# Mixing stage: the triangular inverse kept packed by blocks of 32 up to step 16, its products in four column groups of TensorE, and all spreading copies on ScalarE

## What is computed

```python
def step(state, inp):
    r_t, k_t, v_t, w_t, a_t, b_t = inp
    sa = jnp.einsum('bhvk,bhk->bhv', state, a_t)
    state = state * w_t[:, :, None, :] + sa[..., None] * b_t[:, :, None, :] + v_t[..., None] * k_t[:, :, None, :]
    return state, jnp.einsum('bhvk,bhk->bhv', state, r_t)
```

## Time and profile before

| | us |
|---|---|
| Median of 3 runs | 2895.5 |
| Lowest and highest run | 2890.79, 2899.98 |
| The profiled execution: its own time | 2889.8 |
| The profiled execution: its span | 2888.0 |
| Mean granted clock of PE over the span | 0.97 of full speed |

### The profile page before, as it was taken

One profiled execution on the slowest core, in us unless ns is written; L12 is line 12 of the kernel. 1 busy time (PEld: TensorE's weight loads), 2 busy tenths in 40 slices (PEclk: granted clock), 3 DMA queues, 4 the chain that ended last, 5 costly groups with the idle time before them and its releaser, 6 DMA issues. The chain is left out here.

```text
span 2888.0 us, 38654 instructions
## 1 busy us (share of the span) xinstructions
PE 2693.2 (93%) x14472; PEld 2220.4 (77%) x14473; DVE 1942.9 (67%) x2438; ACT 1350.8 (47%) x1914; POOL 577.5 (20%) x487
## 2 busy tenths in 40 slices
PE   8999988889988879999999699999999899999998
PEld 7988767777776758888888588766677688888887
DVE  4441167777764579999999663586778888887314
ACT  5111155555543257777777452236654334333312
POOL 0000035655550010000000330130000343341000
PEclk9999989999998979999999799999999999999999
DMA  6456111111006459999999631001031222223314
GB/s 205 177 191 251 74 58 54 44 37 36 28 9 232 185 208 408 408 412 409 408 411 368 208 110 47 22 1 60 1 111 63 62 87 87 80 80 116 136 48 160
DMA packets 166286, 439.86 MB, mean 152 GB/s; under 512 B 21852, under 2 KB 102800, under 8 KB 152848
## 3 DMA queue, kind: packets, MB, share of 16 engines
q1 hardware_dynamic: 151552, 384.13, 36.2%
q0 software_dynamic: 8848, 33.03, 3.0%
q10 hardware_dynamic: 5760, 20.97, 1.8%
HBM read 358.93 MB, written 79.17 MB: 152 GB/s over the span
## 5 line engine op out<-in xcount | busy, mean ns | idle before, releaser
L134 PE MATMUL psum<-part,expert_x_high 128*128 128x512 f32 x520 | 207.5, 399 | 2.9 <-issue 1.5
L136 PE MATMUL psum<-part,expert_x_low 128*128 128x512 f32 x520 | 203.8, 392 | 0.0
L134 PE MATMUL psum<-project_w_high,high 128*128 128x448 f32 (+1 forms) x512 | 194.4, 380 | 4.0 <-DVE low L398 4.0
L136 PE MATMUL psum<-project_w_high,low 128*128 128x448 f32 (+1 forms) x512 | 193.5, 378 | 0.0
L135 PE MATMUL psum<-project_w_low,high 128*128 128x448 f32 (+1 forms) x512 | 193.5, 378 | 0.0
L129 DVE TENSOR_TENSOR expert_down_low<-expert_down,expert_down_high 128x2048 fp32r<-128x2048 f32 x62 | 139.3, 2288 | 39.6 <-ACT expert_down_high L124 39.6
L971 POOL TENSOR_TENSOR mix_ab_step<-mix_abrb,mix_pair_mask 128x512 f32<-128x512 f32 x80 | 115.4, 1467 | 182.8 <-ACT mix_abrb L1106 182.4
L129 DVE TENSOR_TENSOR expert_gate_low<-expert_gate,part 128x2048 fp32r<-128x2048 f32 x64 | 143.9, 2289 | 10.0 <-ACT part L124 8.5
L134 PE MATMUL psum<-part,ffn_w_high 128*128 128x512 f32 x352 | 139.9, 397 | 11.4 <-DVE ffn_u L4172 6.3
L129 DVE TENSOR_TENSOR expert_up_low<-expert_up,part 128x2048 fp32r<-128x2048 f32 x64 | 143.8, 2289 | 1.0 <-ACT part L124 1.0
L135 PE MATMUL psum<-ffn_b_low,ffn_w_high 128*128 128x512 f32 x352 | 138.9, 395 | 0.0
(11 more groups left out here) (728 smaller groups left out, 7567.2 us busy)
## 6 DMA issues: line engine op xcount, KB each, us to landing
expert_gate<-in_w_gate_dram SPq DMA_DIRECT2D x32, 2048.0 KB
expert_up<-in_w_up_dram SPq DMA_DIRECT2D x32, 2048.0 KB, 10.2
expert_down<-in_w_down_dram SPq DMA_DIRECT2D x32, 2048.0 KB, 10.9
ffn_w<-in_ffn_w_up_dram SPq DMA_DIRECT2D x44, 512.0 KB, 4.3
y_rows<-expert_y ACTq DMA_DIRECT2D x32, 512.0 KB, 11.0
hidden_rows<-ffn_hidden SPq DMA_DIRECT2D x20, 512.0 KB, 2.8
ffn_hidden<-hidden_rows SPq DMA_DIRECT2D x20, 512.0 KB, 4.1
down_w<-in_ffn_w_down_dram SPq DMA_DIRECT2D x39, 256.0 KB, 2.7
```

The lines of the kernel that those rows point to most:

```text
L134: pe.matmul(out, left[0], right[0], start=start, stop=False)
L136: return pe.matmul(out, left[1], right[0], start=False, stop=stop)
```

## The change

- The inverse of the 32x32 diagonal blocks is kept packed: the four blocks of a head stand below each other on the 128 partitions, 32 columns a head, so that 8 heads are 128x256 instead of 128x1024. DVE packs A's blocks (`pk`, 8 copies of 32 partitions x 128), and the masks of steps 1 to 16 are applied in that form: the first by DVE, four by POOL (128x256 each, `pb`), in place of ten of 128x512.
- For the products one operand is spread to a block-diagonal 128x128 form (`xe`, `ze`; zeroed once). The copies from PSUM that spread it are four per operand, one for each 32 partitions (32x8x32), all on ACT (`ACT_BLOCKS = range(BLOCKS)`): `spread_z` and `spread_n`.
- Each product of steps up to 16 has 32 output partitions. `grow` and `reach_back` issue 8 of them, 4 for each group, at the four column groups of the array. The identity and the products of `grow` accumulate in PSUM (bank 0), so that DVE's adds go.
- `turn_n` transposes the packed inverse (2 transposes instead of 8); ACT takes it out first (`nf`), DVE copies the turned one (`tf`, 128x256).
- Step 32 (`half`) is 16 + 24 products of 32x32x32 with 8 transposes for `x_t`; step 64 (`whole`) is 8 + 8 products of 64x64x64 as before. DVE copies the last part in place of adding it, and clears a part of `xe`.
- The filling work of all engines is put between the new parts: on DVE `tildes_rk` (L713, L714) comes after the last copy of the solve instead of before it; `squash` on ACT moves behind `q1`.
- Constants: one packed mask and `fold` in place of six masks.

```diff
             def score(t):
                 for gr in range(2):
                     v.wait_ge(b_scored, t * 2 + gr + 1)
-                    v.tensor_tensor(x_t[gr][:], two_banks(4 * gr)[:, :, 0, :], per_block(pair_mask[0][:], HG), ALU.mult)\
-                        .then_inc(x_started, 1)
-                    v.wait_ge(x_started, t * 2 + gr + 1)
-                    v.tensor_tensor(x_t[gr][:], x_t[gr][:], per_block(ident[:], HG), ALU.add).then_inc(x_ready, 1)
+                    for b in range(BLOCKS):
+                        v.tensor_copy(pk[leaf(b), gr, :, :], two_banks(4 * gr)[leaf(b), :, 0, leaf(b)]).then_inc(ab_packed, 1)
+                v.wait_ge(ab_packed, (t + 1) * 2 * BLOCKS)
+                v.tensor_tensor(every(pb[0]), every(pk), per_block(packed_mask[:, leaf(0)], 2 * HG), ALU.mult).then_inc(pair_ready, 1)
...
+            def spread_z(t, s):
+                act.wait_ge(z_made, t * NP + s + 1)
+                for b in ACT_BLOCKS:
+                    act.activation(every(ze)[leaf(b), :, leaf(b)], packed(z_bank(s))[leaf(b)], ACT.Copy).then_inc(z_by_act, 1)
+
+            def spread_n(t, s):
+                act.wait_ge(n_made, t * NP + s + 1)
+                for b in ACT_BLOCKS:
+                    act.activation(every(xe)[leaf(b), :, leaf(b)], packed(0)[leaf(b)], ACT.Copy).then_inc(n_by_act, 1)
+                if s < NP - 1:
+                    act.activation(flat(nf[:]), bank[0][:, 0:PACKED], ACT.Copy).then_inc(n_folded, 1)
...
+                spread_n(t, 1)
+                spread_z(t, 2)
+                if not last:
+                    sigmoids(*after)
+                spread_n(t, 2)
+                spread_z(t, 3)
+                if not last:
+                    reach_ends(t + 1, 1 - u)
+                spread_n(t, 3)
+                if not last:
+                    decays(*after)
+                spread_z(t, 4)
+                spread_n(t, 4)
...
+            def unit(t):
+                pe.wait_ge(ab_ready, t * 2 + 1)
+                for gr in range(2):
+                    for b in range(BLOCKS):
+                        pe.matmul(bank[0][leaf(b), gr * P:(gr + 1) * P], fold[:], ident[:], start=(gr == 0), stop=False,
+                                  skip_group_check=True)
+
+            def grow(t, s):
+                pe.wait_ge(z_by_act, (t * NP + s + 1) * len(ACT_BLOCKS))
+                if s:
+                    pe.wait_ge(t_ready, t * (NP - 1) + s)
+                pe.sem_inc(pe_passed, 1)
+                for gr in range(2):
+                    for b in range(BLOCKS):
+                        last = pe.matmul(bank[0][leaf(b), gr * P:(gr + 1) * P], tf[:, gr, b, :] if s else fold[:], ze[:, gr, b, :],
+                                         start=False, stop=(s == NP - 1), skip_group_check=True)
+                last.then_inc(n_made, 1)
+
+            def reach_back(t, s):
+                wait_n(t, s)
+                pe.wait_ge(steps_ready, t * (NP - 1) + s)
+                pe.sem_inc(pe_passed, 1)
+                for gr in range(2):
                     for h in range(HG):
+                        last = pe.matmul(bank[z_bank(s)][leaf(h), gr * P:(gr + 1) * P], pb[s][:, gr, h, :], xe[:, gr, h, :],
+                                         start=True, stop=True)
+                last.then_inc(z_made, 1)
...
+            def turn_n(t, s):
+                pe.wait_ge(n_folded, t * (NP - 1) + s)
...
+                for gr in range(2):
+                    last = pe.transpose(bank[4][:, gr * P:(gr + 1) * P], nf[:, gr, :], ident[:])
+                last.then_inc(n_turned, 1)
...
+            def half(t, fill):
+                wait_n(t, NP)
+                pe.sem_inc(pe_passed, 1)
+                for gr in range(2):
+                    for h in range(HG):
+                        for b in (0, 2):
+                            last = pe.matmul(packed(1)[leaf(b + 1), gr * HG + h, :], abrb[gr][leaf(b), h, 0, leaf(b + 1)],
+                                             xe[leaf(b), gr, h, leaf(b)], start=True, stop=True)
...
+                take_half(t)
+                if not first:
+                    rw_divide(t - 1, rw_link)
+                place_half(t)
+                if not last:
+                    tildes_ba(*after)
+                place_last(t)
+                if not last:
+                    tildes_rk(*after)
...
+            v.memset(xe[:], 0.0).then_inc(zeroed, 1)
+            v.memset(ze[:], 0.0).then_inc(zeroed, 1)
```

More of the change, by code:

```diff
@@ L837, in turn @@
                 score(t)
[L838 to L865 removed]
+                if not last:
+                    kk_link = scale_kk(*after)
@@ new lines, in turn @@
+                if not last:
+                    square_kk(kk_link)
+                take_t(t, 1)
+                scale_state(t, u, first)
+                if not last:
+                    sigmoid_args(*after)
+                take_t(t, 2)
+                if not last:
+                    unit_kk(*after, kk_link)
+                if not last:
+                    divide_kk(kk_link)
+                mask_k(t, 1)
+                take_t(t, 3)
+                if not last:
+                    rated_link = rated(*after)
@@ new lines, in turn @@
+                spread_n(t, 3)
+                if not last:
+                    decays(*after)
+                spread_z(t, 4)
+                spread_n(t, 4)
+                if not last:
+                    decay_before(*after)
+                take_x_t(t)
+                take_half(t)
+                if not first:
+                    rw_deviation(t - 1)
+                    act.wait_ge(ret_ready, t - 1)
+                act.wait_ge(ret_in_ready[u], j * 32 + 32)
+                act.activation(gate[u][:], ret_in[u][:, 3 * RET_W:4 * RET_W], ACT.Silu).then_inc(gate_ready, 1)
@@ L1144, in turn @@
+                act.wait_ge(q_turned, t + 1)
+                act.activation(q1[:], bank[7][:], ACT.Copy).then_inc(q1_ready, 1)
+                if not (isinstance(j, int) and j == PAIRS - 1):
+                    squash(j + 1, u)
                 act.wait_ge(u_made, t + 1)
@@ L1268, in double, with whole @@
+            def whole(t, fill):
+                pe.wait_ge(placed_by_dve, t * 2 + 2)
+                pe.sem_inc(pe_passed, 1)
                 for gr in range(2):
[L1269 to L1271 removed]
                     for h in range(HG):
[L1273 to L1278 removed]
@@ L1281, in raise_state @@
+                for gr in range(2):
+                    for h in range(HG):
+                        n = gr * HG + h
+                        last = pe.matmul(bank[0][FIRST_HALF, n * RW_N:(n + 1) * RW_N], z_last[SECOND_HALF, n, :],
+                                         x_t[SECOND_HALF, gr, h, SECOND_HALF], start=True, stop=True)
+                last.then_inc(last_made, 1)
             def raise_state(t, last_turn):
@@ L1390, in turn @@
                 score_b(t, first)
-                for s in range(NS):
-                    double(t, s, fill)
+                fill("scored")
+                pair(t)
+                unit(t)
+                fill("pair")
+                grow(t, 0)
+                fill("grown0")
+                for s in range(1, NP):
+                    reach_back(t, s)
+                    turn_n(t, s)
+                    fill(f"left{s}")
+                    grow(t, s)
+                    fill(f"grown{s}")
+                half(t, fill)
+                fill("placed")
+                whole(t, fill)
                 pe.wait_ge(q_t_ready, t + 1)
```

357 lines of the change are left out of this document (170 added, 187 removed).

## The result

The changed kernel takes **2929.3 us** (median of 4 runs, 2925.1 to 2932.3), the kernel before, on the same chip, 2896.5: a ratio of 1.012 with a 95% interval of [1.010, 1.014]. The forecast was 2862, its range 2840 to 2896. So the kernel is slower by 33 us, where a gain of 34 was forecast, and the prediction is wrong in its sign.

The account below looks back on a forecast made before the run. Bound: the mixing stage's closed PE-ACT ring, PE nearly full. Turn: 62.05 - 8.9 + 1.7 + 1.3 + 0.8 = 57.0 us; all turns -34, so 2856 profiled and 2862 as median; range 2840 to 2896.

Parts of the forecast that it names:

- steps 32 and 64: End of the solve: products, transposes, ACT copies, table loads, last z copy and DVE's copy and clearing; together 11 us.
- PE's work: Mixing stage: eight 32-column products take 0.8 us (bounds 0.6 to 2.0); PE falls from 55.7 to about 43 us a turn.
- rival 1: Solve products: the four column groups do not overlap, eight products take 2.0 us for 0.8; 2912 us, chance 0.13.
- The ring: Solve loop of PE products and ACT copies with waits: 2.25 us half a step, 4.5 a whole one, before 6.27.
- Rival 4: PE in the mixing stage: changes of product shape empty PE, 2.1 us a turn; 2879 us, chance 0.07.
- One spell of lower clock a turn stays, as now, and slightly more often (+0.5 to +1; below): Mixing turn: lower-clock spells hardly increase; entered in the turn's sum as +0.8 us.
- Rival 3: PE's clock falls in four more stretches a turn, each costing about 1 us; 2894 us, chance 0.09.
- a copy of 32 partitions x 256 has the same length per partition, so I take the same: ACT's spreading copies: 0.38 us each, next start 0.27 later, so four cost 1.2 us.
- Rival 2: ACT's spreading copies are dearer, 0.1 us each for about 45 a turn, 2.4 us a turn; 2881 us, chance 0.11.
- Given back: +1.7: DVE's L713 and L714 now stand after the solve, ahead of the retention mask and tail: +1.7 us a turn.
- +1.3 and +0.8: Added to the step-by-step walk of the turn: +1.3 us for what it misses, +0.8 for lower-clock spells.
- Reach, +1.6: Steps 2 to 16: step 8's `xe` is queued on ACT behind the exponential for `reach`, which waits for PE's sums: +1.6 us.

Follow-up runs that it names:

- experiment 9: Changed kernel with ACT's four spreading copies all in the first 32 partitions (inverse not computed) plus 29 unread PE products a turn: 2846.0 us.
- experiment 5: Changed kernel with each ACT spreading copy over all 128 partitions, times a per-partition factor of 1 or 0, no added products: 2929.6 us.
- experiments 6: Changed kernel with ACT's spreading copies over all 128 partitions with a 1-or-0 factor, plus 29 unread PE products a turn: 2874.7 us.
- 8: Changed kernel with ACT's four spreading copies all in the first 32 partitions (inverse not computed), no added products: 2893.0 us, one run.
- experiment 7: Changed kernel with the spreading copies shared by ACT and DVE, plus 29 unread PE products a turn: 2860.6 us.
- experiment 11: Shared-copies kernel, 26 added products: one running-sum product moved behind step 16's z, ACT copying step 8's n before waiting for reach: 2853.7 us.
- experiments 1: Changed kernel with 18 unread 128x128 PE products a turn, placed where PE waits for ACT's spreading copies: 2901.1 us.
- 3: Changed kernel with spreading copies shared by ACT and DVE, plus 18 unread PE products a turn: 2877.6 us.
- experiment 2: Changed kernel with two of each four spreading copies moved from ACT to DVE, no added products: 2896.6 us.
- experiment 10: Shared-copies kernel with 29 added products, and tildes_rk moved back ahead of the solve's last copy: 2880.0 us.

## Why the prediction was wrong, point by point

| us of the model turn | predicted | after | both conditions met (9) |
|---|---|---|---|
| solve to the end of step 16 | 29.5 | 38.3 | 29.6 |
| steps 32 and 64 | 11 | 12.8 | 12.0 |
| tail and what was added | 16.4 | 16.5 | 13.6 |
| turn | 57.0 | 67.6 | 55.3 |

The first row runs from the first `pk` copy (570.27; 543.54) to the end of the last spread of n (608.56; 573.17), the second to the end of L788 (621.36; 585.18).

- **PE's work: right, on the safe side.** Eight products in four column groups take 0.65 us at full clock (predicted 0.8, bounds 0.6 to 2.0), so rival 1 is out. The Trainium skill (TensorE: Matmul & The Clock Gate, Part 3) would have weight loads overlap running products only if the row group differs; these share all rows, and the trace shows no such cost. PE is busy 47.8 us in a turn at full clock with 29 added products; at 0.25 each (the six ahead of `whole` last 1.50) that leaves some 40.5 for the 43 predicted.
- **The ring: right but for the copies.** With the copies at 1.17 and the clock up, 29.6 us stand against 29.5, opening, waits and table loads included. A part of the closeness is luck: from one `xe` to the next, step 2 takes 5.4 us for the 4.5 of the walk (the added products stand in front of its growth until 555.51, while `ze` is ready at 554.45), and steps 4 to 16 with `nf` are 0.7 cheaper together. Rival 4, the changes of shape, had no term in this sum, and the sum leaves no room for one; no run tries it alone.
- **The step that failed first: "One spell of lower clock a turn stays, as now, and slightly more often (+0.5 to +1; below)".** There are three spells, half of the turn. The rows for it were on the table (PE busy 1.16 of 3.2 us ahead of a stretch at 0.52), and the forecast had just taken 12 us a turn from PE. Rival 3 named it and had two thirds of the size, 4 us a turn for the 6.2 of experiments 5 and 6, but gave it 0.09. The price was also taken from the ring's products alone, 1 us a stretch. A spell runs on into work that keeps PE full, where every product of it is on the path: the tail's L1526 lost 1.5 us by itself.
- **The second: "a copy of 32 partitions x 256 has the same length per partition, so I take the same".** The length is the same (0.37); the spacing is not, since 0.27 was that of copies on the same partitions. Four take 1.57. Rival 2 had it, priced at 2.4 us a turn; 3.5 to 3.8 were measured (experiments 6 and 9, after and 8).
- **The rivals were treated as exclusive.** Both came true. From 55.7, 3.5 for the copies and 6.2 for the clock lead to experiment 5 (65.3), from which both prices are taken; its copies take 1.57 us as those of the changed kernel do, and the 1.0 us a turn between it and the changed kernel (66.3) is not explained. A rival for each term needs a case in which two of them hold; that case lay at 2862 + 19 + 32 = 2913, outside the range.
- **"Given back: +1.7": right in kind, too large.** The two operations have room before PE needs the mask, but DVE's later work has none: in experiment 9 DVE has no wait from the solve's last copy to the turned operands. From the end of that copy to the mask it takes 1.9 us (529.92 to 531.83) and to the first `pk` 11.7 more; before, 0.6 and 11.9. That is 1.1 us. PE now waits for DVE's update of the state, as it did not before. PE's timeline, first of the kernel before, then of experiment 7:

```profile
560.79 0.63 PE L1210 MATMUL psum<-ident,mix_tilde_k 128*128 128x128 f32 x4
```

```profile
543.61 0.63 PE L1299 MATMUL psum<-ident,mix_tilde_k 128*128 128x128 f32 x4 [0.86 <-DVE mix_state L952]
```

- **The other additions, +1.3 and +0.8.** The table counts them with the tail, where they are not found: of the 3.8 us added there 1.1 came. Steps 32 and 64 took 1.0 more than the walk, which is near the 1.3. The 0.8 was for more spells, and these are absent in experiment 9 (clock 0.96, before 0.95); so of the 1.3 us between 57.0 and 55.7 that term alone is 0.8. That the tail of the changed kernel (16.5) agrees with 16.4 is luck: its products ran at the lower level, which made up for what was too dear.
- **Reach, +1.6: the size right, the reason half.** From one `xe` to the next, step 8 takes 5.9 us in experiment 9 and step 16, which is plain, 4.4. But the copy queued behind `reach` does not end the wait: it ends at 568.79, and PE passes at 569.27 from the running sums to step 16's z without a gap. The sums on PE set it, and taking one product out of them gave 1.0 us a turn (experiment 11).

**Not settled.** In one turn, where the loop of two turns goes around, PE stands with nothing to wait for. Before, that was 2.03 us in the profile, after it comes twice:

```profile
636.13 0.63 PE L1278 MATMUL psum<-ident,mix_tilde_b 128*128 128x128 f32 x4 [1.75 <-issue]
...
641.07 1.08 PE L1278 MATMUL psum<-ident,mix_tilde_k 128*128 128x128 f32 x4 [3.43 <-issue]
```

The second stall is absent in experiments 1 and 3 and is 3.8 us in experiment 7. Where the instructions lie differs between these kernels, but so does the work, so neither is shown to be the cause. That turn takes 73.2 us, for 67.6 and 71.0 of its neighbours, so it is about a tenth of the 33 us that had to be explained. What sets it was not tried. Nor was the kernel before run with added products: it has spells of its own (0.52 after PE had been busy 1.16 of 3.2 us), so how much of the 1.3% of experiment 11 belongs to the change and how much to the added products is open.

## What to carry to other kernels

Thinning the busiest engine is not free when that engine's speed depends on being busy: before forecasting a gain from less of PE's work, mark each idle stretch that the new order leaves it, and price the stretch behind it at the lower level for all of PE's work there, the untouched too. Where such stretches remain, products that nobody reads, placed ahead of waits, can be worth more than the change itself (here 19 us, experiment 2 to 3, to 55 us, experiment 5 to 6). And when two rivals are about different terms of the sum, add them before setting the range.

## What was not expected of the hardware

- Copies of ACT start 0.27 to 0.28 us apart when they stay on the same partitions, 32 or 128 of them, and 0.40 apart, after the end of the one before, when each is on another quarter. DVE does not overlap them either (its timeline in experiment 7): two copies of 32x256, 0.42 each, take 0.88 on two quarters, while L745, on all partitions like L744 ahead of it, starts 0.08 before L744 has ended.

```profile
549.66 0.88 DVE L776 COPY mix_ze<-psum 32x256 f32<-32x256 f32 x2 [0.53 <-PE psum L1326]
```

- A spell at the lower level outlasts its cause: 3.4 us with PE nearly idle were followed by 9.9 us at 0.50 in which it was busy 96% of the time.
- The same operation of DVE with two operands in SBUF (L744, L745) took 1.75 us while POOL worked (experiment 10) and 0.69 while it did not (the changed kernel), so a gap in DVE's timeline is worth less than its length if POOL works in it.
